# Who loads the w_down pieces: one load queue or two in the expert stage of a mixture-of-experts layer

## The chip, the cores and the metric

The kernel runs on one core of a Trainium2 chip. The metric is the device time of one execution in microseconds (us), as the median of several runs.

## What is computed

One decoder layer in f32 for 512 tokens of width 1024: a mixer (matrix-memory heads and a gated MLP that share an input and an output projection), then a mixture of 32 experts, of which every token uses 4, then a final norm. The change lies in the loads of the expert stage alone:

```
xb  = x[toks]                          # the tokens of one block of one expert
hb  = xb @ w_up[e] + b_up[e]           # 1024 -> 2048
act = min(glu,7) * sigmoid(1.702*glu) * (clip(lin,-7,7) + 1)
yb  = (act @ w_down[e] + b_down[e]) * gate      # 1024 -> 1024
y[toks] += yb
```

Each expert has 12.58 MB of weights (w_up 8.39 MB, w_down 4.19 MB), all of which are read from HBM once: 403 MB in total.

## The kernel before

The mixer and the router take the first 310 us or so. Then the tokens are cut into blocks of 32 rows by expert; an expert that has n tokens takes ceil(n/32) blocks, and at least one. For the inputs of this case there are 78 blocks.

**The order of experts.** Two weight buffers W0 and W1 in SBUF take turns; the text calls the turn of an expert its *position*, 0 to 31, and its buffer is the position's parity `par`. Experts 0 and 1 stand at positions 0 and 1 (their weights are loaded before the router is done). The others are sorted by load on VectorE, and light and heavy ones alternate, the most uneven pairs first. A table `order_tab` holds the expert of each position, `base_tab` the number of blocks before it. In blocks the positions hold 3, 2, 1, 5, 1, 4, 1, 4, 1, 4, 2, 3, then 2 and 3 in turn up to position 27, and 2, 2, 2, 1 at the end (counted in the trace: one L1047 per block, one L1089 per position).

**Pieces.** A weight buffer is cut into six pieces of 2 MB (128 partitions of 16 KB): pieces 0 to 3 are w_up, here called u0 to u3, pieces 4 and 5 are w_down, here d4 and d5. `load_piece` (L299 to L307) issues one; it lands on its own semaphore `s_w[par][n]`. `load_bias_up` (L309) and `load_bias_dn` (L314) load 8 KB and 4 KB of bias.

**TensorE (L1366 to L1414).** `block_up` does 64 matmuls (L1376) that need u0 to u3 in turn, and tells with `m_u[0..3]` when each piece has been read. `block_down` does 64 matmuls (L1391) for the block before it; after the first half it counts `m_yh` (d4 has been read), after the second `m_y` (d5 has been read). The order on TensorE is up(g), down(g-1), up(g+1), down(g), also across experts: the last block of one expert does its down part behind the first up part of the next.

**VectorE (L1041 to L1100).** Per block it adds the bias (L1047, counts `m_z`), clips, multiplies, transposes; L1064 adds the down bias out of PSUM, L1066 multiplies by the gate and counts `m_ys`. L1078 transposes the next block's tokens. **ScalarE (L670 to L672)** does one sigmoid a block: it waits for `m_gl` from L1049. **GpSimd (L499 to L539)** gathers the tokens of a coming block (L506) and scatters the result of the last (L515), both as indirect DMAs of 128 KB.

**SyncE issues every weight load, in one order (L384 to L402).** For each position from 2 on it goes through the pieces 0 to 5. Before each it waits until the former user of the buffer has read that piece (`m_u`, `m_yh`, `m_y`), before the biases also for `m_z` and `m_ys`, and from the third piece on for the landing of the piece two before it (`AHEAD = 2`):

```
for n in range(6):
    sp.wait_ge((*m_u, m_yh, m_y)[n], done)
    ...
    if n >= AHEAD:
        sp.wait_ge(s_w[par][n - AHEAD], 16 * i + 16)
    load_piece(sp, par, n, e)
```

At the end SyncE loads the residual rows (L411), waits for the last scatter, loads all results (L415), and the four tiles of 128 tokens are summed, normed and stored.

Of the kernel before, what the change touches and what calls it, by code (L numbers as in the profile page):

```python
# [30 lines left out]
ALU = mybir.AluOpType  # L31
ACT = mybir.ActivationFunctionType
# [10 lines left out]
NE = 32  # L43
TOPK = 4
BT = 32
NBMAX = T * TOPK // BT + NE
# [4 lines left out]
ALPHA = 1.702  # L51
# [4 lines left out]
def hybrid_layer(nc, x, norm1_gain, w_in, conv_qk, b_igate, b_fgate, mlstm_norm_gain, gmlp_ln_gain,  # L56
# [3 lines left out]
    with ctx:  # L60
# [31 lines left out]
        order_tab = sb("order_tab", [P, NE], i32)  # L92
        base_tab = sb("base_tab", [P, NE + 3], i32)
# [12 lines left out]
        z = m(512)  # L106
        sg, aT = m(256), m(256)
# [205 lines left out]
        def load_bias_dn(eng, par, e):  # L313

            src = b_down[0, e].rearrange("e (j c) -> (e j) c", j=H)
            eng.dma_start(bias_dn[par][0:P:BT, :], src).then_inc(s_bd[par], 16)
# [4 lines left out]
        @block.sync  # L321
        def _(sp):
            def load_x(c):
                sp.dma_start(xin[:, c, :], x[0, P * c:P * (c + 1), :]).then_inc(s_tile[c], 16)

            def load_group(slot, c0):
                sp.dma_start(grp[slot], wcols(c0)).then_inc(s_grp[slot], 16)

            load_x(0)
            load_x(1)  # L330
            load_group(VG, 1024)
            load_x(2)
            load_x(3)
            load_group(QG, 0)
            sp.wait_ge(s_const, 5)
            sp.dma_start(wg[:, :, 0:8], w_in[0, :, 2048:2056].rearrange("(k p) n -> p k n", p=P)).then_inc(s_wg, 16)
            for slot, c0 in ((KG, 512), (OG, 1536), (VGG, 2568), (UG, 2056)):
                load_group(slot, c0)
            sp.wait_ge(s_proj, 12)
            sp.dma_start(wo, w_out[0].rearrange("(k p) n -> p k n", p=P)).then_inc(s_wo, 16)  # L340
            sp.wait_ge(s_wt, NT)
            sp.dma_start(n2row, norm2_gain.broadcast_to([P, D])).then_inc(s_n2row, 16)
            sp.wait_ge(s_proj, 24)
            for c in range(NT):
                sp.dma_start(xres[:, c, :], x[0, P * c:P * (c + 1), :]).then_inc(s_xres, 16)

            def first(par, n):
                load_piece(sp, par, n, slice(par, par + 1))

            first(0, 0)  # L350
            first(0, 1)
            sp.wait_ge(s_p, NT * H)
            sp.wait_ge(s_hm, NT)
            sp.wait_ge(s_hg, NT)
            first(1, 1)
            for c in range(NT):
                if c == NT - 2:
                    sp.wait_ge(s_hTe, 2 * NT)
                    first(0, 5)
                if c == NT - 1:  # L360
                    sp.wait_ge(s_out, 2 * NT)
                    first(0, 2)
                    sp.wait_ge(s_bz, 1)
                    for par in range(2):
                        load_bias_up(sp, par, slice(par, par + 1))
                        load_bias_dn(sp, par, slice(par, par + 1))
                sp.wait_ge(s_hs, c + 1)
                rows = slice(P * H * c, P * H * (c + 1))
                sp.dma_start(hres[rows, :].rearrange("(p j) n -> p (j n)", j=H), xres[:, c, :]).then_inc(s_rowst[c], 16)
                sp.dma_start(hsrow[rows, :].rearrange("(p j) n -> p (j n)", j=H), HS[:, c % 2, :])\  # L370
                    .then_inc(s_rowst[c], 16)
            first(0, 3)
            sp.wait_ge(s_lge, NT)
            first(1, 5)
            for c in range(NT):
                sp.wait_ge(s_rowst[c], 32)
            first(0, 4)
            first(1, 0)
            first(1, 4)
            sp.wait_ge(s_gtab, 1)  # L380
            sp.wait_ge(s_trash, 32)
            first(1, 2)
            first(1, 3)
            with sp.Fori(1, NE // 2) as i:  # L384
                for par in range(2):
                    e = bass.ts(sp.value_load(order_tab[0:1, bass.ts(2 * i + par, 1)], min_val=0, max_val=NE - 1), 1)  # L386

                    done = sp.value_load(base_tab[0:1, bass.ts(2 * i + (par - 1), 1)], min_val=1, max_val=NBMAX - 1)  # L388
                    for n in range(6):
                        sp.wait_ge((*m_u, m_yh, m_y)[n], done)  # L390
                        sp.nop(nofuse=True)
                        if n == 1:
                            sp.wait_ge(m_z, done)
                            sp.nop(nofuse=True)
                            load_bias_up(sp, par, e)
                        if n == 4:
                            sp.wait_ge(m_ys, done)
                            sp.nop(nofuse=True)
                            load_bias_dn(sp, par, e)
                        if n >= AHEAD:  # L400
                            sp.wait_ge(s_w[par][n - AHEAD], 16 * i + 16)
                        load_piece(sp, par, n, e)  # L402

            done = sp.value_load(base_tab[0:1, NE - 1:NE], min_val=1, max_val=NBMAX - 1)
            sp.wait_ge(m_y, done)
            sp.nop(nofuse=True)
            sp.dma_start(grow, final_gain.rearrange("(a n) -> a n", a=1).broadcast_to([P, D]))\
                .then_inc(s_late, 16)
            for c in range(NT):
                rows = slice(P * H * c, P * H * (c + 1))  # L410
                sp.dma_start(hfin[:, c, :], hres[rows, :].rearrange("(p j) n -> p (j n)", j=H)).then_inc(s_tile[c], 16)  # L411
            sp.wait_ge(f_ready, 1)
            for c in range(NT):
                rows = slice(P * H * TOPK * c, P * H * TOPK * (c + 1))
                sp.dma_start(yfin[:, c, :], yrow[rows, :].rearrange("(p r) n -> p (r n)", r=H * TOPK))\  # L415
                    .then_inc(s_tile[c], 16)
            for c in range(NT):
                sp.wait_ge(f_y, c + 1)
                sp.dma_start(out[0, P * c:P * (c + 1), :], hfin[:, c, :]).then_inc(f_out, 16)
            sp.wait_ge(f_out, 16 * NT)  # L420
# [129 lines left out]
        def _(act):  # L550
# [116 lines left out]

            act.wait_ge(s_tab, 1)
            total = act.value_load(base_tab[0:1, NE:NE + 1], min_val=NE, max_val=NBMAX - 1)
            with act.Fori(0, total) as g:  # L670
                act.wait_ge(m_gl, g + 1)
                act.activation(sg, z[:, 0:256], ACT.Sigmoid, scale=ALPHA).then_inc(m_sg, 1)  # L672

            for c in range(NT):
                act.wait_ge(f_sum, c + 1)
# [6 lines left out]
        def _(dve):  # L682
# [251 lines left out]
            for c in range(NT):  # L934
                residual(c, 0)
                if c + 1 < NT:
                    cat_evac(c + 1)
                if c >= 1:
                    norm_evac(c - 1)
                    top_experts(c - 1)  # L940
                residual(c, 1)
                if c == NT - 1:
                    norm_evac(c)
                second_norm(c)
                if c == 0:
                    dve.wait_ge(s_rc, 8)
                    V.tensor_copy(iota_f, iota_i)
                    V.tensor_copy(iota16, iota_i)
                    V.tensor_copy(tokm, tokm_i)
                    V.tensor_copy(spread16, ident[0:BT, 0:BT].unsqueeze(1).broadcast_to([BT, H, BT]))  # L950
                    V.tensor_copy(spread, ident[0:BT, 0:BT].unsqueeze(1).broadcast_to([BT, H, BT]))
                    V.tensor_scalar(part_i[:, 1:2], part_i[:, 0:1], 5, None, ALU.logical_shift_right)
                    link(V.tensor_scalar(part_i[:, 2:3], part_i[:, 0:1], 31, None, ALU.bitwise_and))
                    link(V.tensor_copy(partf[:, 1:3], part_i[:, 1:3]))
                    link(V.tensor_scalar(partf[:, 3:4], partf[:, 1:2], float(T * TOPK * H), None, ALU.add))
                    V.tensor_scalar(partf[:, 2:3], partf[:, 2:3], float(H), None, ALU.mult)
                    link(V.tensor_copy(partf[:, 0:1], part_i[:, 0:1]))
                    link(V.tensor_scalar(late[:, 1:2], partf[:, 0:1], 1.5, 4096.0, ALU.is_lt, ALU.mult))
                    V.tensor_tensor(late[:, 1:2], late[:, 1:2], partf[:, 0:1], ALU.subtract)
                    link(V.tensor_scalar(expb, ones, partf[:, 0:1], None, ALU.mult))  # L960
            top_experts(NT - 1)

# [145 lines left out]
            def base(e):  # L1108

                return dve.value_load(base_tab[0:1, bass.ts(e, 1)], min_val=1, max_val=NBMAX - 1)  # L1110
# [335 lines left out]
```

## Time and profile before

| | us |
|---|---|
| median of 3 runs | 1337.59 (1337.36 to 1339.75) |
| the profiled execution | 1336.38 |
| its span in the profile | 1334.5 |
| TensorE matmul busy | 1140.2 (85%) |
| VectorE busy | 489.4 (37%) |
| ScalarE busy | 200.0 (15%) |
| GpSimd busy | 225.2 (17%) |
| moved by DMA | 463.78 MB |

Times within the trace are us from the start of the span. A line as L306 is a line of the kernel before. "SPq" rows are DMA issues on SyncE's queue; the time beside such a row with "x2" or "x3" runs from the first issue of the group to the end of the last, waits between them included. "GB/s" is what all 16 DMA engines moved, and the DMA share is the mean busy share of these engines. Of all DMA queues the one of SyncE is q1 and GpSimd's is q0; ScalarE's is q10.

### The profile page before, as it was taken

Reading aid. Unit: us, or ns where it says so; the run is one execution under the profiler, and the core shown is the slowest. Engines: PE = TensorE matmul, PEld = TensorE weight load, DVE = VectorE, ACT = ScalarE, POOL = GpSimd, SP = SyncE. Lnnn points to the kernel's source line nnn. Section 1 sums busy time; section 2 is a strip of 40 time slices with the busy share of each in tenths; the row PEclk is TensorE's granted clock in tenths of the full one; section 3 lists DMA queues with packets and bytes.
Section 4 is the critical chain, followed back from the end, with each engine's and each line's share of the span. In section 5 each row is a group of like instructions: output and inputs, shape, how many; then the busy total and the mean of one; then the engine's idle time right before and its main releaser. Section 6 shows DMA issues by size and latency. Waiting matters only on the chain.

```text
span 1334.5 us, 28532 instructions
## 1 busy us (share of the span) xinstructions
PE 1140.2 (85%) x10978; PEld 526.0 (39%) x10979; DVE 489.4 (37%) x1224; ACT 200.0 (15%) x297; POOL 225.2 (17%) x392
## 2 busy tenths in 40 slices
PE   7999999976979997979998979879798989798740
PEld 3445554543434442433443424333333434343220
DVE  2283462443323332433433323333332333233217
ACT  2114321011111111111111111111111111111101
POOL 2000022001112221212221212121221212121113
PEclk9999999986989998999999999998998999998885
DMA  9303005349699999999999999999999999999987
GB/s 346 117 1 126 16 1 225 153 174 413 253 414 425 391 425 427 425 427 425 426 425 426 426 427 426 420 424 425 425 426 425 420 428 415 424 426 425 427 352 300
DMA packets 51088, 463.78 MB, mean 348 GB/s; under 512 B 9052, under 2 KB 10264, under 8 KB 25976
## 3 DMA queue, kind: packets, MB, share of 16 engines
q1 hardware_dynamic: 41184, 441.89, 79.4%
q0 software_dynamic: 7632, 20.85, 4.0%
q10 hardware_dynamic: 2248, 0.71, 0.2%
q8 instruction: 16, 0.26, 0.1%
q14 instruction: 8, 0.07, 0.0%
HBM read 446.65 MB, written 16.78 MB: 347 GB/s over the span
## 4 chain that ended last, share of the span: by engine, by line
DMA 56%; PE 29%; SPq 5%; DVE 5%; issue 3%; ACT 0%; POOL 0%; ACTq 0%; POOLq 0%; DVEq 0%
DMA W<-in_w_up_dram 54%; PE B L1151 11%; PE B L1376 8%; PE B L1272 4%; PE B L1391 3%; SPq L306 2%; SPq L311 1%; SPq L386 1%; DMA W<-yrow 1%; SPq L388 1%; DMA yrow<-misc,idx_s 1%; DMA misc<-hsrow,idx_g 1%; DVE W L1123 1%; PE B L1295 0%; PE B L1167 0%
## 5 line engine op out<-in xcount | busy, mean ns | idle before, releaser
L1376 PE MATMUL B<-W,misc 128*32 128x512 f32 x4992 | 590.4, 620 | 117.6 <-DMA W<-in_w_up_dram 82.0
L1376 PEld LDWEIGHTS B<-W,misc 128*32 128x32 f32 x4992 | 184.3, 112 | 473.9 <-issue 464.3
L1391 PE MATMUL B<-W,misc 128*32 128x256 f32 x4992 | 289.7, 383 | 2.5 <-DMA W<-in_w_down_dram 1.6
L1391 PEld LDWEIGHTS B<-W,misc 128*32 128x32 f32 x4992 | 189.6, 112 | 126.9 <-issue 56.0
L1047 DVE TENSOR_TENSOR misc<-B,misc 128x512 f32<-128x512 f32 x78 | 53.9, 691 | 418.5 <-PE B L1376 418.5
L1151 PE MATMUL B<-W 128*128 128x512 f32 x384 | 169.5, 597 | 0.0
L672 ACT ACTIVATE misc<-misc 128x256 f32<-128x256 f32 x78 | 32.5, 416 | 839.8 <-DVE misc L1049 839.8
L503 POOL COPY idx_g<-idx_tab 128x1 uint32 (+1 forms) x79 | 15.0, 190 | 596.5 <-DVE misc L1078 577.7
L1151 PEld LDWEIGHTS B<-W 128*128 128x128 f32 x384 | 72.0, 192 | 84.6 <-issue 84.6
L515 POOL DMA_INDIRECT yrow<-misc,idx_s x78 | 78.4, 1006 | 148.4 <-DVE misc L1066 148.4
L672 ACT ACT_TABLE_LOAD x78 | 100.1, 1283 | 4.8 <-DVE idx_tab L1024 3.5
L506 POOL DMA_INDIRECT misc<-hsrow,idx_g x79 | 77.8, 985 | 62.3 <-POOL idx_g L503 30.1
L1064 DVE TENSOR_TENSOR misc<-B,misc 128x256 f32<-128x256 f32 x78 | 33.0, 423 | 92.9 <-POOL idx_s L511 77.2
L1073 DVE STREAM_TRANSPOSE misc<-misc 128x256 f32<-128x256 f32 x78 | 34.6, 444 | 69.9 <-PE B L1391 69.9
L1272 PE MATMUL B<-W 128*128 128x512 f32 x128 | 57.8, 609 | 0.1
L1055 DVE TENSOR_TENSOR misc<-misc 128x256 f32<-128x256 f32 x78 | 48.5, 622 | 2.7
L1272 PEld LDWEIGHTS B<-W 128*128 128x128 f32 x128 | 24.5, 195 | 29.6 <-issue 29.6
L443 POOL TENSOR_SCALAR misc<-misc 128x1 f32<-128x1 f32 (+1 forms) x20 | 5.3, 264 | 173.7 <-ACT W L639 80.4
L1078 DVE STREAM_TRANSPOSE misc<-misc 128x256 f32<-128x256 f32 x79 | 33.5, 423 | 2.0 <-DMA misc<-hsrow,idx_g 2.0
L1052 DVE SCALAR_TENSOR_TENSOR misc<-misc 128x256 f32<-128x256 f32 x78 | 33.2, 425 | 2.7
L1066 DVE TENSOR_SCALAR misc<-misc,gate_tab 128x256 f32<-128x256 f32 x78 | 27.6, 353 | 11.0
L1049 DVE TENSOR_SCALAR misc<-misc 128x256 f32<-128x256 f32 x78 | 22.9, 294 | 2.7
(267 smaller groups left out, 487.0 us busy)
## 6 DMA issues: line engine op xcount, KB each, us to landing
W<-in_w_up_dram SPq DMA_DIRECT2D x128, 2048.0 KB, 11.6
W<-in_w_down_dram SPq DMA_DIRECT2D x64, 2048.0 KB, 9.8
W<-in_w_in_dram SPq DMA_DIRECT2D x6, 2048.0 KB, 18.9
W<-yrow SPq DMA_DIRECT2D x4, 2048.0 KB, 14.7
W<-in_x_dram SPq DMA_DIRECT2D x8, 512.0 KB, 5.0
W<-in_w_out_dram SPq DMA_DIRECT2D x1, 4096.0 KB, 12.8
hres<-W SPq DMA_DIRECT2D x4, 512.0 KB, 3.1
hsrow<-W SPq DMA_DIRECT2D x4, 512.0 KB, 4.0
```

Source lines behind the costliest of these rows:

```text
L506: pool.indirect_dma_start(out=xg, out_offset=None, in_=hsrow, in_offset=bass.IndirectOffsetOnAxis(ap=idx_g[:, 0:1], axis=0))\
L515: pool.indirect_dma_start(out=yrow, out_offset=bass.IndirectOffsetOnAxis(ap=idx_s[:, 0:1], axis=0), in_=ysb, in_offset=None).then_inc(m_sc ...
L672: act.activation(sg, z[:, 0:256], ACT.Sigmoid, scale=ALPHA).then_inc(m_sg, 1)
L1047: V.tensor_tensor(z, B[0][:], bias_up[par], ALU.add).then_inc(m_z, 1)
L1052: V.scalar_tensor_tensor(lin, lin, 1.0, glu, ALU.add, ALU.mult).then_inc(m_t, 1)
L1055: V.tensor_tensor(glu.rearrange("p (m r i) -> p m i r", m=2, r=4), lin.rearrange("p (m i r) -> p m i r", m=2, r=4), sg.rearrange("p (m i r ...
L1073: V.transpose(aT, z[:, 0:256]).then_inc(m_aT, 1)
L1078: V.transpose(xT, xg).then_inc(m_xT, 1)
L1151: ins = mm(B[n % 2][:], lhs(k), rhs(k), start=(k == 0), stop=(k == NK - 1))
L1272: ins = mm(B[n][:], HT[:, c % 2, k, :], wo[:, k, 512 * n:512 * (n + 1)], start=(k == 0), stop=(k == NK - 1))
L1376: ins = mm(B[0][BT * j:BT * (j + 1), :].rearrange("p (g h c) -> p g h c", g=2, h=2), xT[:, BT * k:BT * (k + 1)], up(par)[:, k, :, :, P * j ...
L1391: ins = mm(B[5][BT * j:BT * (j + 1), 0:QC], aT[:, BT * q:BT * (q + 1)], down(par)[:, q, QC * j:QC * (j + 1)], start=(q == 0), stop=(q == N ...
```

## The change

SyncE keeps pieces 0 to 3 and the up bias. ScalarE issues pieces 4 and 5 and the down bias on its own queue, between its sigmoids, without the wait for an earlier piece's landing. For this its one loop over all blocks is cut into one loop per position. The rule that sorts the experts on VectorE gets two other operations in place of two, which also order experts 0 and 1 among themselves; for these inputs it gives the same order.

```diff
-                    for n in range(6):
-                        sp.wait_ge((*m_u, m_yh, m_y)[n], done)
+                    for n in range(4):
+                        sp.wait_ge(m_u[n], done)
                         sp.nop(nofuse=True)
                         if n == 1:
                             sp.wait_ge(m_z, done)
                             sp.nop(nofuse=True)
                             load_bias_up(sp, par, e)
-                        if n == 4:
-                            sp.wait_ge(m_ys, done)
-                            sp.nop(nofuse=True)
-                            load_bias_dn(sp, par, e)
                         if n >= AHEAD:
                             sp.wait_ge(s_w[par][n - AHEAD], 16 * i + 16)
                         load_piece(sp, par, n, e)
...
-            with act.Fori(0, total) as g:
-                act.wait_ge(m_gl, g + 1)
-                act.activation(sg, z[:, 0:256], ACT.Sigmoid, scale=ALPHA).then_inc(m_sg, 1)
+            def base(e):
+                return act.value_load(base_tab[0:1, bass.ts(e, 1)], min_val=1, max_val=NBMAX - 1)
+            def sigmoids(first, last):
+                with act.Fori(first, last) as g:
+                    act.wait_ge(m_gl, g + 1)
+                    act.activation(sg, z[:, 0:256], ACT.Sigmoid, scale=ALPHA).then_inc(m_sg, 1)
+            sigmoids(0, base(1) + 1)
+            with act.Fori(1, NE // 2) as i:
+                for par in range(2):
+                    e = bass.ts(act.value_load(order_tab[0:1, bass.ts(2 * i + par, 1)], min_val=0, max_val=NE - 1), 1)
+                    done = base(2 * i + (par - 1))
+                    act.wait_ge(m_yh, done)
+                    act.nop(nofuse=True)
+                    load_piece(act, par, 4, e)
+                    act.wait_ge(m_y, done)
+                    act.nop(nofuse=True)
+                    load_piece(act, par, 5, e)
+                    act.wait_ge(m_ys, done)
+                    act.nop(nofuse=True)
+                    load_bias_dn(act, par, e)
+                    sigmoids(done + 1, base(2 * i + par) + 1)
...
-                    link(V.tensor_scalar(late[:, 1:2], partf[:, 0:1], 1.5, 4096.0, ALU.is_lt, ALU.mult))
-                    V.tensor_tensor(late[:, 1:2], late[:, 1:2], partf[:, 0:1], ALU.subtract)
+                    link(V.tensor_scalar(late[:, 1:2], partf[:, 0:1], -2.0, 0.0, ALU.add, ALU.min))
+                    V.scalar_tensor_tensor(late[:, 1:2], late[:, 1:2], -4096.0, partf[:, 0:1], ALU.mult, ALU.subtract)
```

On SyncE's queue, one even position (buffer W0) before; s_w0_0 to s_w0_3 are the landings of u0 to u3 of this position:

```order
L306 ISA [waits m_u0]
L306 DMA W0<-in_w_up_dram 128x4096
L311 ISA [waits m_u1,m_z]
L311 DMA misc<-in_b_up_dram 4x4x128
L306 ISA
L306 DMA W0<-in_w_up_dram 128x4096
L401 ISA [waits m_u2]
L306 ISA [waits s_w0_0]
L306 DMA W0<-in_w_up_dram 128x4096
L306 ISA [waits m_u3,s_w0_1]
L306 DMA W0<-in_w_up_dram 128x4096
L316 ISA [waits m_yh,m_ys]
...
L306 ISA [waits s_w0_2]
L306 DMA W0<-in_w_down_dram 128x4096
L306 ISA [waits m_y,s_w0_3]
L306 DMA W0<-in_w_down_dram 128x4096
```

The up part stays as it is; after its last row SyncE's queue now goes on to the next position's table reads and its wait for m_u0. On ScalarE's queue, the same position in the changed kernel (line numbers of the changed kernel, L675 is the sigmoid):

```order
L306 ISA [waits m_yh]
L306 DMA W0<-in_w_down_dram 128x4096
L306 ISA [waits m_y]
L306 DMA W0<-in_w_down_dram 128x4096
L316 ISA [waits m_ys]
L316 DMA misc<-in_b_down_dram 4x256
...
L669 TENSOR_LOAD base_tab
...
L675 ACTIVATE misc<-misc 128x256 [waits m_gl]
```

The w_down pieces now wait only for the reads of the buffer's former user, and no longer for u2 and u3 of their own position.

## Rows read from the trace of the kernel before

**Rows 1.** Busy time by stretch, all engines.

```profile
core 0: us, PE busy (x) PEld busy (x) DVE busy (x) ACT busy (x) POOL busy (x), PEclk, DMA share, GB/s
351.00:402.00 51.00, 39.75 (x460) 17.22 (x452) 16.02 (x42) 5.95 (x7) 9.48 (x16) 0.93 0.99 404
...
441.00:466.00 25.00, 23.38 (x284) 10.67 (x280) 9.37 (x26) 3.40 (x4) 5.74 (x9) 1.00 0.97 388
...
500.00:1250.00 750.00, 656.72 (x7675) 286.29 (x7668) 250.70 (x638) 101.96 (x120) 142.36 (x240) 0.95 1.01 425
```

**Rows 2.** The DMA queues from 500 to 1250 us.

```profile
q1 hardware_dynamic: 21432, 302.69, 95.3%
q0 software_dynamic: 5813, 15.87, 5.4%
...
W<-in_w_up_dram SPq DMA_DIRECT2D x96, 2048.0 KB, 11.6
W<-in_w_down_dram SPq DMA_DIRECT2D x48, 2048.0 KB, 9.9
```

**Rows 3.** What SyncE's queue waited for: us in total, times, longest.

```profile
SPq L306 <- DMA W<-in_w_up_dram: 695.0, 117, 12.0
...
SPq L398 <- DVE misc L1066: 8.8, 3, 4.2
```

**Rows 4.** ScalarE's wait for its sigmoids, and rows of ScalarE and VectorE, 640 to 650 us.

```profile
ACT misc L672 <- DVE misc L1049: 839.8, 78, 21.4
...
644.39 0.35 DVE L1066 TENSOR_SCALAR misc<-misc,gate_tab 128x256 f32<-128x256 f32 x1
...
650.16 0.42 ACT L672 ACTIVATE misc<-misc 128x256 f32<-128x256 f32 x1 [8.60 <-DVE misc L1049]
```

**Rows 5.** Two table reads on SyncE's queue, their first parts, 371 to 373 us.

```profile
371.76 0.05 SPq L386
...
372.60 0.05 SPq L388
```

**Rows 6.** TensorE at position 3 (five blocks); the last column is idle before, and what ended it.

```profile
402.84 1.92 PE L1376 MATMUL B<-W,misc 128*32 128x512 f32 x16 [2.98 <-DMA W<-in_w_up_dram]
...
408.00 7.08 PE L1376 MATMUL B<-W,misc 128*32 128x512 f32 x64
...
418.32 7.08 PE L1376 MATMUL B<-W,misc 128*32 128x512 f32 x64
...
438.96 7.08 PE L1376 MATMUL B<-W,misc 128*32 128x512 f32 x64
```

**Rows 7.** Issues on SyncE's queue for positions 5 (441.13, 447.01) and 31.

```profile
441.13 0.33 SPq L306 DMA_DIRECT2D W<-in_w_up_dram  x1
447.01 0.64 SPq L311 DMA_DIRECT2D misc<-in_b_up_dram  x1
...
1274.71 5.32 SPq L306 DMA_DIRECT2D W<-in_w_down_dram  x2
```

**Rows 8.** Pieces, all of L306: from issue to landing.

```profile
DMA to landing us min/median/max: 7.9/10.4/26.1
```

**Rows 9.** The chain that ended last, its end: start us, us, what.

```profile
1269.25 10.29 DMA W<-in_w_up_dram
1279.68 1.93 PE B L1376 x16
1281.60 3.49 PE B L1391 x64
1287.15 6.35 DMA yrow<-misc,idx_s
1295.65 2.43 DMA yrow<-misc,idx_s
```

**Rows 10.** The scatters, all of L515: from issue to landing.

```profile
DMA to landing us min/median/max: 2.4/6.9/8.4
```

**Rows 11.** What TensorE waited for, the longest.

```profile
PE B L1376 <- DMA W<-in_w_up_dram: 82.0, 32, 3.8
```

More of the change, by code:

```diff
@@ L669, in _ @@
             total = act.value_load(base_tab[0:1, NE:NE + 1], min_val=NE, max_val=NBMAX - 1)
-            with act.Fori(0, total) as g:
-                act.wait_ge(m_gl, g + 1)
-                act.activation(sg, z[:, 0:256], ACT.Sigmoid, scale=ALPHA).then_inc(m_sg, 1)
+            def base(e):
[19 more added lines that the diff above has]
+                    sigmoids(done + 1, base(2 * i + par) + 1)
+            behind_last = base(NE - 1)
+            with act.If_lt(act.to_reg(behind_last + 1), act.to_reg(total)):
+                sigmoids(behind_last + 1, total)
             for c in range(NT):
```

## The prediction

> **What bounds the kernel now.** I read the busy time by stretch first, then the DMA queues, then the waits, then the chain. From 500 to 1250 us the 16 DMA engines are busy for the whole time at 425 GB/s, while TensorE has 657 of 750 us [rows 1]. In that stretch SyncE issues 96 pieces of w_up and 48 of w_down [rows 2]: 750/144 = 5.21 us a piece, 31.3 us a position, whatever TensorE does. TensorE waits for pieces of w_up, 32 times and 82.0 us in all [rows 11]. So the reader should see a stream of 180 pieces (positions 2 to 31) that is the clock of the stage, and compute that hangs on it. SyncE itself is no bound: 695.0 us of its queue's time are waits for a landing [rows 3].
>
> Two places matter more than that average. The first is **the end**. The chain runs through u3 of position 31, which lands at 1279.54 (1269.25 + 10.29), then the last quarter of the up part (1279.68), a down part (1281.60), and two scatters (1287.15 and 1295.65) [rows 9]. d5 of position 31 is issued only at about 1279.7, behind the landing of u3 (the second of the pair that starts at 1274.71) [rows 7], and lands while the chain goes through TensorE and the first scatter. So the last two pieces of the stream are not on the path; the last u3 is. The second is **position 3**, the expert with five blocks. Its u3 lets TensorE go on at 402.84; four more blocks follow, the last up part from 438.96, one block each 10.32 us (418.32 - 408.00) [rows 6]. Only when that last up part has read u0 can SyncE issue u0 of position 5, at 441.13 [rows 7].
>
> **The change, part by part.**
>
> *SyncE loses two pieces, a bias and their waits.* Its waits for m_ys were 8.8 us in three cases [rows 3]. All of that stands beside a DMA stream that is full; worth 0. If the cover went, the most it could give back is what the stream lacks where it is not full: 51 us at 404 instead of 425 GB/s and 25 us at 388 [rows 1], that is 51 x 0.05 = 2.5 and 25 x 0.09 = 2.2, together 4.7 us.
>
> *ScalarE gets 30 times two pieces, a bias and three table reads.* An issue takes 0.33 us on SyncE's queue and a bias 0.64 [rows 7]; a read of a table takes 0.84 us (372.60 - 371.76 [rows 5]). The bias goes behind m_ys, counted by L1066 (644.39 + 0.35); with 0.64 and one read ScalarE is free at 646.2, and its next sigmoid starts at 650.16 after 8.60 us of idle [rows 4]. The rest is done earlier. ScalarE's idle before its sigmoids is 839.8 us for 78 [rows 4], 10.8 us each. Cost 0, with 4 us of cover at each position. The table load of 1.28 us behind each sigmoid goes from the loops; it stood in the same idle time, so 0. VectorE's two exchanged operations on one column each, once: 0.
>
> *The order of the stream changes.* This is the main term. Before, d4 waits for the landing of u2 and d5 for that of u3, so the stream is u0 u1 u2 u3 d4 d5 in each position. After, ScalarE issues d4 of position p+2 when TensorE has done half a down part behind position p+1's first up part. That is 1.9 + 1.7 us after u3 of p+1 has landed (the last quarter of the up part and half of a down part's 3.49 [rows 9]), and d5 1.7 us later. At that time SyncE can have at most u0 and u1 of p+2 on its queue; u2 must wait until u0 has landed, a piece time later. So both d pieces are with the engines before u2 and u3 are. The scatters show how the engines treat two queues: a scatter of 128 KB lands after 2.4 us when nothing else runs, and mostly after 6.9 us beside the weights [rows 10], although whole pieces need 7.9 us at the least [rows 8] and several are queued. It isn't put behind them all; the queues take turns. With turns, both d pieces need at most 4 x 5.21 = 20.8 us from their issue and are in before u3. **u3 becomes the last piece of its position**, 2 x 5.21 = 10.4 us later for the same bytes moved. The Trainium skill ("DMA: Bandwidth & Descriptors", section "Queues, rings and completion order") says that each DMA engine goes round-robin between the queues that have work, packet by packet; the scatters' landing agrees.
>
> At the end this is paid in full: the chain hangs on the last u3, so **+10.4 us**. The bounds are 0 (d pieces still behind u3) and 10.4.
>
> *Position 3 runs the stream dry.* From the landing of u3 (402.84) to the issue of u0 of position 5 (441.13) are 38.3 us, set by TensorE. Before, eight pieces stand between the two (d4 d5 of position 3, six of position 4): 8 x 5.21 = 41.7 us. A piece alone takes 7.9 us from issue to landing [rows 8], 7.9 - 4.9 = 3.0 more than its 2.1 MB at 425 GB/s. 38.3 + 3.0 = 41.3 is just under 41.7: the stream holds, nearly, which is what the 0.97 share there shows [rows 1]. After, d4 and d5 of position 3 are already in, and six pieces remain: 31.3 us. The engines idle for 41.3 - 31.3 = **+10.0 us**. The positions with four blocks (5, 7, 9) free the buffer 10.3 us earlier: 41.3 - 10.3 = 31.0 against 31.3, no dry time, but no margin either. Those with three or fewer have 10 us to spare. Bounds: 0 (order as before) and 10.0 + 3 x 2 = 16, if each four-block position misses by 2 us (its u1 still waits for m_z behind u0: 447.01 against 441.13 is 5.9 us, more than a piece [rows 7]).
>
> *The tail gets lighter.* In the changed kernel nothing of the weights is behind the last u3. The first scatter of the tail took 6.35 us beside d5, the last 2.43 [rows 9], so up to 3.9 us may come back; but the loads of the residual rows, which stood behind d5, now run beside it. I take half: **-2**, bounds -3.9 and 0.
>
> *Gathers and scatters share with a third queue.* One scatter to the next is its landing plus 2.15 us (1295.65 - 1287.15 - 6.35 [rows 9]); with the usual 6.9 [rows 10] that is 9.05 against a block of 10.32 [rows 6], a margin of 1.27 us. One busy weight queue adds 4.5 us (6.9 - 2.4) to a landing. The trace has no stretch with two; the nearest row bounds what the second adds by 0 and 4.5. Where TensorE waits for weights anyway it costs nothing; only the blocks behind the first ones of the heavy positions feel it. I take **+1**, close to the lower end, since most of the stage has slack on TensorE.
>
> **Sum.** 10.4 + 10.0 - 2 + 1 = 19.4 us, made against the profiled execution's 1336.38; the median is 1.2 us above that: 1337.6 + 19.4 = **1357**. The case's own range is 1351 to 1368: below, the third term at -3.9, the fourth at 0, and 3 us off because the d pieces only partly get ahead; above, the second at 16, the third at 0, the fourth at 4.5 (1337.6 + 10.4 + 16 + 4.5).
>
> **Rivals.**
>
> *Faster.* The engines serve SyncE's queue so that the w_up pieces aren't held up by ScalarE's, and ScalarE's pieces fill the holes of the stream, at 351 to 402 and 441 to 466 us: 4.7 us as worked out, 1333. It decides if u3 of a position keeps landing before its d5. For it: the stream has those holes, and SyncE stands at waits in one fixed order. Against it: d4 and d5 are issued before u2 is, and the total is 425 GB/s with or without a second queue beside it (q1 and q0 give 95.3% and 5.4% [rows 2]), so more queues bring no more rate.
>
> *No change.* The stream is full, nothing else changes, and the last d pieces stay off the path: 1337.6, within the 0.2% (2.7 us) that a measurement of this kernel can tell. The Trainium skill, same page, section "Issuing engines are not separate DMA queues", says that starting DMAs from several engines saves only the sequencer's time to initiate them; by that rule alone this rival would be the forecast. What speaks against it is that the order changes, which that rule says nothing of.
>
> *Only the end.* The stream doesn't run dry at position 3, because SyncE issued something I don't see or the d pieces of positions 3 and 4 come late: 1337.6 + 10.4 - 2 = 1346.
>
> *The indirect transfers become the bound.* If the second queue adds the full 4.5 us, a block takes 6.9 + 4.5 + 2.15 = 13.55 us wherever ScalarE's queue is busy, 3.2 more than now. Over the 17 blocks of positions 3, 5, 7 and 9 that is up to 55 us, over the four later blocks of position 3 alone 13; between these I take 25: 1382. It decides above 1.27 us of extra landing time. For it: the margin is that thin. Against it: TensorE has slack behind position 10.
>
> **Chances.** Forecast 0.64, only the end 0.11, indirect transfers 0.12, faster 0.08, no change 0.05. The range takes in forecast and "only the end", and the half of the indirect case that costs less: 1344 to 1376, with 0.08 + 0.05 + 0.07 left out. Faster by over 0.2%: 0.08; within: 0.05; slower: 0.87.
>
> **What would show it.** Right: DMA issues on ScalarE's queue, each d pair issued before its u2; the wait of TensorE for w_up grown; a stretch of about 10 us between 430 and 460 us in which the DMA share falls to near 0; then 425 GB/s again; the last u3 landing at about 1300, with no weight landing after it, and 53 us from there to the end. Wrong: the DMA share at position 3 unbroken (second term), d5 landing behind the last u3 (first term), or the scatters' median landing above 8.2 us with blocks apart by more than 10.3 us (fourth term). A rate other than 425 GB/s in the middle would upset the whole sum: each per cent is 9 us.

## The result, and the profile after

| | before | changed |
|---|---|---|
| median of 4 runs, us | 1337.47 (1336.98 to 1339.75) | 1357.21 (1356.79 to 1357.39) |
| ratio, 95% interval | | 1.0145 (1.0129 to 1.0162) |
| span of the profiled execution | 1334.5 | 1355.6 |

The changed kernel is slower by 19.7 us, where 19.4 were forecast. First its busy time by stretch (columns as in rows 1: us, PE, PEld, DVE, ACT, POOL, TensorE's clock, DMA share, GB/s):

```profile
351.00:402.00 51.00, 38.13 (x440) 16.44 (x432) 16.11 (x42) 1.83 (x4) 9.45 (x16) 0.93 1.00 410
402.00:441.00 39.00, 32.34 (x364) 12.82 (x368) 11.07 (x27) 1.25 (x3) 5.42 (x10) 0.87 1.00 420
441.00:466.00 25.00, 23.84 (x288) 9.70 (x284) 8.96 (x22) 0.83 (x2) 6.41 (x11) 1.00 0.55 201
...
500.00:1250.00 750.00, 658.61 (x7744) 285.14 (x7739) 252.18 (x639) 24.99 (x60) 143.47 (x243) 0.94 1.01 425
```

From 500 to 1250 us the rate has not changed: 425 GB/s as in [rows 1], with the weights on two queues now instead of one. Between 441 and 466 us the DMA share fell from 0.97 to 0.55, 201 GB/s instead of 388: (0.97 - 0.55) x 25 = 10.5 us of the stream lost. Nearly all of it lies between 440 and 452 us, where the share is 0.14:

```profile
440.00:452.00 12.00, 12.00 (x148) 4.86 (x144) 4.22 (x11) 0.42 (x1) 3.54 (x6) 1.00 0.14 53
```

The page's DMA queues show how the weights are divided, and its DMA issues how long a piece now takes from issue to landing (median, last column):

```profile
q1 hardware_dynamic: 32304, 315.94, 56.3%
q10 hardware_dynamic: 11128, 126.66, 22.1%
...
W<-in_w_up_dram SPq DMA_DIRECT2D x128, 2048.0 KB, 18.7
W<-in_w_down_dram ACTq DMA_DIRECT2D x60, 2048.0 KB, 23.2
```

In [rows 2] these medians are 11.6 and 9.9 us, from 500 to 1250 us; in the same stretch of the changed kernel they are 19.4 and 20.5 us. The two queues share the engines, and each piece takes about twice as long. The end of the chain that ended last (start us, us, what):

```profile
1253.15 25.17 DMA W<-in_w_up_dram
1278.47 20.80 DMA W<-in_w_up_dram
...
1299.40 3.64 PE B L1398 x16
1303.05 3.62 PE B L1413 x64
...
1308.73 5.97 DMA yrow<-misc,idx_s
...
1316.85 2.44 DMA yrow<-misc,idx_s
```

The last u3 lands at 1299.27 (1278.47 + 20.80), against 1279.54 in [rows 9]: 19.7 us later. The spans of the two profiled executions differ by 21.1 us (1355.6 - 1334.5); the 1.4 us left over lie behind that landing. (The profiled execution before was 1.1 us shorter than its median, the changed one 0.2 us longer, so the medians differ by 19.7.) No weights move any more from 1299 us on, as the busy time of the next 5 us shows (DMA share 0.00, the column before the last):

```profile
1299.00:1304.00 5.00, 4.60 (x36) 1.69 (x40) 0.86 (x2) 0.00 (x0) 0.18 (x1) 0.58 0.00 0
```

TensorE at position 3, to be read against [rows 6] (L1398 is the up part, L1413 the down part; in brackets the idle time before, and what ended it):

```profile
405.23 3.64 PE L1398 MATMUL B<-W,misc 128*32 128x512 f32 x16 [7.96 <-DMA W<-in_w_up_dram]
412.30 3.59 PE L1398 MATMUL B<-W,misc 128*32 128x512 f32 x16 [3.42 <-DMA W<-in_w_up_dram]
415.69 3.66 PE L1413 MATMUL B<-W,misc 128*32 128x256 f32 x64
419.16 7.05 PE L1398 MATMUL B<-W,misc 128*32 128x512 f32 x64
...
429.48 7.05 PE L1398 MATMUL B<-W,misc 128*32 128x512 f32 x64
...
450.12 7.05 PE L1398 MATMUL B<-W,misc 128*32 128x512 f32 x64
```

u3 of position 3 lets TensorE go on at 412.30 instead of 402.84, 9.5 us later. The last of the five up parts starts 37.8 us after that (450.12 - 412.30; before 438.96 - 402.84 = 36.1). The difference of 1.7 us is the last quarter of the first up part, 3.59 us here and 1.92 before. Only then can u0 of position 5 be issued:

```profile
452.27 0.34 SPq L306 DMA_DIRECT2D W<-in_w_up_dram  x1
```

That is 40.0 us after 412.30, and in this time the stream has six pieces to carry instead of eight.

### The profile page after: what moved, and what is told of

The parts are those of the page before. It is cut to its first block, busy times and chain, and to the rows that moved or that the text cites. A ratio compares the mean times of both kernels' runs of the same rounds, so it can differ in the third digit from the quotient of the medians.

```text
span 1355.6 us, 28875 instructions
## 1 busy us (share of the span) xinstructions
PE 1138.5 (84%) x10978; PEld 519.0 (38%) x10979; DVE 491.2 (36%) x1224; ACT 105.1 (8%) x224; POOL 224.5 (17%) x392
## 4 chain that ended last, share of the span: by engine, by line
PE 53%; DMA 38%; DVE 5%; issue 1%; SPq 1%; ACT 0%; POOL 0%; ACTq 0%; POOLq 0%; DVEq 0%
DMA W<-in_w_up_dram 34%; PE B L1398 24%; PE B L1173 11%; PE B L1413 11%; PE B L1294 4%; DMA W<-in_w_down_dram 2%; DMA W<-yrow 1%; DVE misc L1069 1%; SPq L311 1%; DMA yrow<-misc,idx_s 1%; DMA misc<-hsrow,idx_g 1%; DVE W L1145 0%; DMA W<-in_b_spatial_dram 0%; PE B L1317 0%; PE B L1189 0%
## 5 line engine op out<-in xcount | busy, mean ns | idle before, releaser
L1398 PE MATMUL B<-W,misc 128*32 128x512 f32 x4992 | 585.4, 619 | 134.7 <-DMA W<-in_w_up_dram 98.3
L1398 PEld LDWEIGHTS B<-W,misc 128*32 128x32 f32 x4992 | 182.2, 113 | 485.8 <-issue 475.6
L1413 PE MATMUL B<-W,misc 128*32 128x256 f32 x4992 | 293.0, 386 | 5.1 <-DMA W<-in_w_down_dram 4.2
L1413 PEld LDWEIGHTS B<-W,misc 128*32 128x32 f32 x4992 | 184.9, 113 | 140.3 <-issue 65.2
L675 ACT ACTIVATE misc<-misc 128x256 f32<-128x256 f32 x78 | 32.5, 417 | 955.6 <-DVE misc L1071 955.6
L507 POOL COPY idx_s<-misc 128x1 uint32 (+1 forms) x78 | 14.8, 189 | 60.3 <-DMA yrow<-misc,idx_s 60.0
## 6 DMA issues: line engine op xcount, KB each, us to landing
W<-yrow SPq DMA_DIRECT2D x4, 2048.0 KB, 14.6
```

Source lines behind the costliest of these rows:

```text
L1398: ins = mm(B[0][BT * j:BT * (j + 1), :].rearrange("p (g h c) -> p g h c", g=2, h=2), xT[:, BT * k:BT * (k + 1)], up(par)[:, k, :, :, P * j ...
L1413: ins = mm(B[5][BT * j:BT * (j + 1), 0:QC], aT[:, BT * q:BT * (q + 1)], down(par)[:, q, QC * j:QC * (j + 1)], start=(q == 0), stop=(q == N ...
```

## The experiments

Times below are medians; each ratio is to the kernel before on the same chip, with its 95% interval. A difference of two ratios is turned into us with 1338. A single ratio is good to between 1.4 and 3.6 us by its interval, so the differences to the changed kernel under the next two headings are each good to about 4 us. The runs have names (e1 to e10); the "first" and the "sixth experiment" of an expectation are e1 and e6.

### e2: position 31 alone goes back to SyncE

In this and the next two kernels the body of each loop over positions is a function, and the first and the last pair of positions are written out, so that one position can differ; the rest is the changed kernel.

```diff
+        SYNC_DOWN = (31,)
...
+                for n in range(pieces):
+                    sp.wait_ge((*m_u, m_yh, m_y)[n], done)
...
-                    for n in range(4):
-                        sp.wait_ge(m_u[n], done)
...
+            load_position(NE // 2 - 1, 0, 4)
+            load_position(NE // 2 - 1, 1, 6 if 31 in SYNC_DOWN else 4)
...
+            position(NE // 2 - 1, 0, True)
+            position(NE // 2 - 1, 1, 31 not in SYNC_DOWN)
```

The third argument is the number of pieces that SyncE loads, and on ScalarE whether it loads w_down.

> The changed kernel, but at position 31 alone SyncE issues d4 and d5 behind u2 and u3, as before. Theory (the last u3 is the end of the path): 10.4 us less than the changed kernel, 1346 to 1348, the last u3 landing at about 1289, the dry stretch at position 3 unchanged. Rival (only the total of the stream counts, the order at the end is hidden): 1357, no change.

Measured: 1349.14 us, ratio 1.0074 (1.0048 to 1.0101). Against the 1.0145 of the changed kernel that is 0.0071 x 1338 = 9.5 us less, a little short of the 10.4 that was expected. The dry stretch is as it was (0.55). The chain of this kernel:

```profile
1248.13 20.84 DMA W<-in_w_up_dram
1269.11 3.64 PE B L1419 x16
1272.75 4.18 PE B L1434 x64
1276.93 6.87 PE B L1419 x64
1283.80 3.45 PE B L1434 x64
...
1287.77 7.07 PE B L1419 x64
1294.84 3.49 PE B L1434 x64
```

The chain no longer ends in the u3 of position 31, but in that of position 30 (1248.13 + 20.84 = 1268.97), from where TensorE works with hardly a break (0.5 us): u0 to u3 of position 31 are in before it comes to them. So the order at the end does cost time, and what is next behind the last u3 is the u3 of position 30, late for the same reason. That the 10.4 us show as 9.5 fits this, but the difference is less than these times can tell.

### e3: position 3 alone goes back to SyncE

```diff
+        SYNC_DOWN = (3,)
...
+            load_position(1, 1, 6 if 3 in SYNC_DOWN else 4)
...
+            position(1, 1, 3 not in SYNC_DOWN)
```

> The changed kernel, but at position 3 alone (five blocks) SyncE issues d4 and d5 behind u2 and u3. Theory: the stream no longer runs dry at position 3, the DMA share from 441 to 466 us goes from 0.55 back to 0.95 or more, and 10 us go: 1346 to 1349. Rival (the dry stretch only moves to another heavy position, or was hidden in TensorE's slack): 1354 to 1357.

Measured: 1347.91 us, ratio 1.0068 (1.0043 to 1.0092), 0.0077 x 1338 = 10.3 us less than the changed kernel. Its busy time by stretch:

```profile
402.00:441.00 39.00, 38.04 (x464) 15.56 (x468) 14.40 (x35) 1.67 (x4) 7.25 (x13) 0.96 1.01 424
441.00:466.00 25.00, 23.27 (x286) 9.80 (x280) 9.63 (x25) 0.83 (x2) 5.91 (x10) 1.00 0.93 371
```

TensorE is busy for 38.0 of 39 us again (32.3 in the changed kernel), and the DMA share is back at 0.93, a little under the 0.95 that was expected. The rival fell. No run has the first and last pairs written out with nothing moved back; that this alone changes nothing is argued from the traces (e2 keeps the dry stretch, e3 the late last u3) and from the next run.

### e4: both go back to SyncE

```diff
+        SYNC_DOWN = (3, 31)
```

> The changed kernel with d4 and d5 of positions 3 and 31 on SyncE, behind u2 and u3; the other 28 positions stay on ScalarE. Theory: both terms go and they add: 1336 to 1340, the time of the kernel before. Rival (the second queue costs something of its own all along, through slower scatters and gathers): 1341 to 1347 remain.

Measured: 1338.40 us, ratio 0.9998 (0.9988 to 1.0009). Two of 30 positions moved back, and the whole loss is gone: 9.5 + 10.3 = 19.8 against 19.7. The other 28 positions keep the second queue, with all that it does to gathers and scatters, and cost nothing that can be measured (the interval reaches 1.6 us below the kernel before and 1.2 us above it). Their stretch still reads 425 GB/s:

```profile
500.00:1250.00 750.00, 656.37 (x7744) 287.40 (x7740) 253.93 (x641) 25.06 (x60) 143.62 (x243) 0.95 1.01 425
```

### e5: turns or age

```diff
-        AHEAD = 2
+        AHEAD = 4
```

> The changed kernel with AHEAD = 4: SyncE issues u0 to u3 as soon as the buffer's former user has read them, with no wait for an earlier landing. In light positions all four are then issued before ScalarE's d4 and d5. If the engines take turns between the two queues: the d pieces still get half the rate and are in before u3, so 1355 to 1358, as the changed kernel. If they serve by age of issue: u3 lands ahead of d4 and d5 in the light positions, the last u3 about 10 us earlier, 1344 to 1350.

Measured: 1358.65 us, ratio 1.0149 (1.0128 to 1.0171): as the changed kernel. The issues for position 31, SyncE's and then ScalarE's (the third of the three up pieces ends at 1255.38):

```profile
1253.91 1.47 SPq L306 DMA_DIRECT2D W<-in_w_up_dram  x3
```

```profile
1275.60 1.78 ACTq L306 DMA_DIRECT2D W<-in_w_down_dram  x2
```

and the chain:

```profile
1255.05 45.10 DMA W<-in_w_up_dram
1300.28 3.64 PE B L1398 x16
```

u3 was issued 20 us ahead of d4 and landed 45 us after its issue, at 1300.15, at the end of the stream. Had the engines served by age, it would have been in before both d pieces. Service by age is ruled out: the two queues take turns. But d5 isn't in before u3 either, as the expectation had it: it was issued at 1277.03 and landed 23.3 us later, at 1300.3. Both queues run out together. The Trainium skill ("DMA: Bandwidth & Descriptors", section "Queues, rings and completion order") says that an engine goes round between the queues that have work; by it the time stays, and the run agrees.

### e1 and e7: one queue in the new order

```diff
-                    for n in range(6):
+                    turn = (0, 1, 4, 5, 2, 3)
+                    for k, n in enumerate(turn):
...
-                        if n >= AHEAD:
-                            sp.wait_ge(s_w[par][n - AHEAD], 16 * i + 16)
+                        if k >= AHEAD:
+                            sp.wait_ge(s_w[par][turn[k - AHEAD]], 16 * i + 16)
```

> The kernel before, with SyncE alone issuing everything, but in the order u0 u1 d4 d5 u2 u3 in each position; ScalarE issues nothing. Theory (the order of the stream is the cause): u3 is again the last piece of its position, so about 10 us at the end and about 10 us dry time at position 3 come as in the changed kernel: 1354 to 1359, the DMA share between 441 and 466 us near 0.55, the last u3 landing at about 1299. Rival (the second queue is the cause: turns between queues, ScalarE's issues, slower gathers and scatters): 1337 to 1340.

Measured: 1456.33 us, ratio 1.0886 (1.0859 to 1.0912). Neither theory gave this number. What SyncE's queue waited for (us in total, times, longest; L1392 is the down part, L1067 counts m_ys):

```profile
SPq L392 <- PE B L1392: 308.9, 30, 11.6
...
SPq L399 <- DVE misc L1067: 128.3, 30, 7.0
```

SyncE now stands at m_yh and m_ys in each of the 30 positions with only u0 and u1 queued, 10.4 us of work, for (308.9 + 128.3) / 30 = 14.6 us on average, and the stream runs dry: from 500 to 1250 us its DMA share is 0.94 and it moves 387 GB/s. The next run, e7, took the wait for m_ys away from there, by putting the down bias behind u3.

```diff
-                        if n == 4:
-                            sp.wait_ge(m_ys, done)
-                            sp.nop(nofuse=True)
-                            load_bias_dn(sp, par, e)
...
                         load_piece(sp, par, n, e)
+                    sp.wait_ge(m_ys, done)
+                    sp.nop(nofuse=True)
+                    load_bias_dn(sp, par, e)
```

> As the first experiment (SyncE alone, order u0 u1 d4 d5 u2 u3), but the down bias with its wait for m_ys goes behind u3 instead of ahead of d4. If that run's extra 100 us came from SyncE standing at m_ys with only two pieces queued behind it, the wait gone leaves the order alone: the DMA share from 500 to 1250 us is back at 1.0, and the time is 1354 to 1362. If waiting for m_yh and m_y alone is enough to drain two pieces: 1380 to 1450.

Measured: 1399.16 us, ratio 1.0440 (1.0413 to 1.0467), 405 GB/s in that stretch. So the wait for m_ys was about half of it (118 us lost with it, 59 without), and the waits for m_yh and m_y drain the queue by themselves:

```profile
SPq L392 <- PE B L1391: 343.7, 55, 12.0
```

These two don't separate order from queue, since a second mechanism came in: on one queue a late wait holds back every piece behind it. So no run shows the new order without the second queue; what speaks against the second queue as the cause is e4, in which 28 positions keep it at no cost. What e1 and e7 do show is what ScalarE's own queue is good for: with w_down issued between u1 and u2 one queue costs 59 us, while the two queues cost 20.

### e8, e6, e9 and e10: SyncE's waits, and the tail

```diff
-        AHEAD = 2
+        AHEAD = 4
```

> The kernel before with AHEAD = 4 instead of 2. If SyncE's landing waits leave holes in the stream (it is idle for 3.2 us between 356 and 1280 us in the kernel before), 1335 to 1337; if the stream is full whatever SyncE does, 1337 to 1339; if a deeper queue slows gathers and scatters, above 1339.

Measured: 1338.32 us, ratio 0.9997 (0.9983 to 1.0011). The stream is full with SyncE's landing waits or without most of them.

The other edit to the kernel before moves the residual rows behind the last scatter:

```diff
-            for c in range(NT):
-                rows = slice(P * H * c, P * H * (c + 1))
-                sp.dma_start(hfin[:, c, :], hres[rows, :].rearrange("(p j) n -> p (j n)", j=H)).then_inc(s_tile[c], 16)
             sp.wait_ge(f_ready, 1)
             for c in range(NT):
...
                     .then_inc(s_tile[c], 16)
+                rows = slice(P * H * c, P * H * (c + 1))
+                sp.dma_start(hfin[:, c, :], hres[rows, :].rearrange("(p j) n -> p (j n)", j=H)).then_inc(s_tile[c], 16)
```

> The kernel before, with the four loads of the residual rows issued behind the last scatter, each behind the result rows of its tile, instead of ahead of it. If these loads hold up the two scatters of the tail: the first of them lands after 2.4 to 4 us instead of 6.35, the end comes 1 to 3 us earlier, 1334.5 to 1337. If d5 alone holds it up: the scatter stays at 6 us and the result rows come up to 1.2 us later for it, 1338 to 1340.

Measured: 1337.86 us, ratio 1.0003 (0.9989 to 1.0017), no gain. Its profile is read from e9, the same kernel once more.

> The kernel of the sixth experiment once more, for its profile. If the residual rows hold up the first scatter of the tail, it lands after 2.4 to 4 us; if d5 does, after 6 us or more. The time as there, 1335 to 1339.

Measured once: 1338.79 us. The first scatter of the tail (L514) and what follows it on GpSimd:

```profile
1289.99 0.99 POOL L514 DMA_INDIRECT yrow<-misc,idx_s  x1 [11.70 <-DVE misc L1065]
1292.72 0.18 POOL L510 COPY idx_s<-misc 128x1 uint32 x1 [1.73 <-DMA yrow<-misc,idx_s]
```

It landed within 2.7 us of its issue, against 6.35 in [rows 9]: in the kernel before, too, it was mainly the residual rows that held it up. (d5 was still in flight for about 1 us of it here and 2.4 us there.) The chain now goes through d5, which has come onto the path:

```profile
1281.26 9.70 DMA W<-in_w_down_dram
...
1291.10 1.97 PE B L1390 x32
...
1294.77 2.44 DMA yrow<-misc,idx_s
```

The same edit to the changed kernel:

> The changed kernel with the same edit: the residual rows behind the last scatter. No weight is behind the last u3 here, so the first scatter of the tail has the engines for itself: it lands after 2.4 to 3 us instead of 5.97, the end comes 2 to 3 us earlier than the changed kernel, 1354 to 1355.5. If the scatter stays at 6 us something else than the loads holds it up, and the time is 1357 to 1359.

Measured: 1359.01 us, ratio 1.0159 (1.0143 to 1.0176), not faster than the changed kernel; the 2 to 3 us that were expected to go did not. The chain:

```profile
1310.28 2.45 DMA yrow<-misc,idx_s
...
1314.88 2.43 DMA yrow<-misc,idx_s
...
1321.12 24.93 DMA W<-hres
1346.08 2.30 DVE W L1144
```

The scatter does land in 2.45 instead of 5.97 us: the residual rows were what it shared with. But these 3.5 us are given back: the residual rows are now loaded together with the result rows, and the last of them lands at 1346.05, where the last result rows of the changed kernel land at 1342.25. No version tried here beats the kernel before.

## Why the prediction was right, point by point

**What bounds the kernel: right.** 425 GB/s before and after, and 426 with a deeper queue (e8). The Trainium skill ("DMA: Bandwidth & Descriptors", section "Issuing engines are not separate DMA queues") says that the issuing engines share the same 16 DMA engines, and the rate agrees; its conclusion, that only issue time is saved, would have given no change. The order that pieces land in is what it leaves out.

**u3 becomes the last piece: right in what it costs at the end, wrong in its picture.** The step had both d pieces "with the engines before u2 and u3", and in before u3, after 20.8 us at most. Position 31 of the changed kernel: u2, then d4 and d5, then d5 alone with its time from issue to landing:

```profile
1273.48 0.33 SPq L306 DMA_DIRECT2D W<-in_w_up_dram  x1
```

```profile
1274.88 1.57 ACTq L306 DMA_DIRECT2D W<-in_w_down_dram  x2
```

```profile
1276.11 0.34 ACTq L306 DMA_DIRECT2D W<-in_w_down_dram  x1
```

```profile
DMA to landing us min/median/max: 23.3/23.3/23.3
```

d4 was issued 1.4 us behind u2 and 3.6 us ahead of u3 (1278.47), and d5 landed at 1299.4, 0.2 us behind u3 (1299.27). So two signs came out against the prediction: "each d pair issued before its u2", and "d5 landing behind the last u3", which it had named as a sign that the term is wrong. Nor was position 31 an exception: of the 30 positions, d4 was issued ahead of u2 in 7, and d5 landed behind u3 in 20. d4 came later than the step had it, 6.4 us instead of 3.6 us after the landing of the u3 before (1268.48 in this trace). 1.7 us of that are the quarter in between, which took 3.64 us behind a wait of 7.33 (see the last section); what makes up the rest stays open.

What holds is less than the step said, and enough: from 1275 us on u2 and u3 share the engines with d4 and d5, so the last u3 is not in before the whole stream is. Before, it was in two pieces, 10.4 us, ahead of the end of the stream. 10.4 is thus the most that the term can be, and both queues ran out together, so that it was reached. The prediction took this bound for a reason that the trace doesn't bear out; in so far its size is luck. Undone alone (e2) the term measured 9.5 us.

**Position 3 runs dry: right.** 10.0 us forecast. Lost in that stretch: 10.5 us by the DMA share; undone alone (e3): 10.3. Of the 19.7 us by which the last u3 lands later, 19.7 - 10.4 = 9.3 are left for it. Here d4 and d5 are in before u3 (409.7 and 412.2 us), as the first step had it. It left out that TensorE needs 40.0 instead of 38.3 us from there to the release of u0, 1.7 us more, the slower quarter behind the wait; by its own sum that makes 40.0 + 3.0 - 31.3 = 11.7. That 41.3 against 41.7 us is only just enough before, and 31.0 against 31.3 for four blocks after, held too: the DMA share is 1.01 from 500 to 1250 us, where the buffers of positions 5, 7 and 9 come free.

**The tail gets lighter: wrong.** -2 us was forecast. From the landing of the last u3 to the end of the span are 1355.6 - 1299.27 = 56.33 us, against 1334.5 - 1279.54 = 54.96: +1.4. The first scatter takes 5.97 instead of 6.35 us, because it shares with the residual rows (e10, and e9 for the kernel before), hardly with d5; and the last quarter of the up part takes 3.64 instead of 1.93 us (see the last section), which the prediction did not have. The step "up to 3.9 us may come back" took d5 for what the scatter shares with.

**Gathers and scatters: +1 us was forecast, and nothing of it can be seen.** All scatters of the changed kernel, from issue to landing:

```profile
DMA to landing us min/median/max: 2.4/8.7/11.4
```

The median is 1.8 us above [rows 10], over the 8.2 that was named as a warning and beyond the margin of 1.27. Yet 28 positions with the second queue cost nothing in e4. The other half of that warning did not come: the blocks behind the first of position 3 are 10.32 us apart (429.48 - 419.16), as before, although d4 and d5 of position 4 were issued on ScalarE's queue at 419.08 and landed at 434.6 and 443.0. The longest scatter of all, 11.4 us, lies in this stretch. So the prediction's rule, that a landing plus 2.15 us must fit into one block, does not hold for a single scatter. How many late ones in a row it would take, no run shows.

**The other costs at 0: right.** ScalarE's busy time fell from 200.0 to 105.1 us, because the table load behind each sigmoid went, and this moved nothing; its waits before the sigmoids are 955.6 us now.

**The sum.** Forecast 10.4 + 10.0 - 2 + 1 = 19.4, measured 19.7. The two main terms carry it: 9.5 + 10.3 by the experiments (each good to about 4 us), 0.0147 x 1338 = 19.7 for both together (e4, good to about 3). That the sum is right to 0.3 us is luck. Between the two profiles the last u3 moved by 19.7 us where 20.4 were forecast and the tail by +1.4 where it was -2, a miss of 3.4; the +1 us for gathers and scatters did not show; and of the 21.1 us that this makes, the medians show 19.7, since the profiled execution before was a short one.

## What to carry to other kernels

When one stream of loads is the clock of a stage, count what each consumer needs last. Moving a part of the loads to another queue added no rate here (425 GB/s either way); the queues take turns, and the pieces that were last and off the path now share the engines with those that are on it, which land later for it. Before such a move, look at the two places where the stream has a boundary: its end (what lands last, and does the chain wait for it?), and the longest stretch in which no buffer comes free (how many pieces are queued for it, against how long it lasts).

A single queue with mixed conditions is no free answer either: pieces whose release comes late must stand behind enough others. Two pieces of 5.2 us were too few here for waits of 14.6 us on average (e1, m_yh and m_ys together).

## What the runs showed of the hardware that was not expected

**TensorE's clock after a wait.** Before, TensorE waited 3.8 us at most for a piece [rows 11]; after, less often and up to 8.0:

```profile
PE B L1398 <- DMA W<-in_w_up_dram: 98.3, 20, 8.0
```

The last quarter of the last up part, 16 matmuls, took 1.93 us before and 3.64 after. Before, the granted clock was 1.00 there:

```profile
1279.00:1284.00 5.00, 4.32 (x65) 2.56 (x69) 2.24 (x6) 0.42 (x1) 0.00 (x0) 1.00 1.01 433
```

After, it is 0.58 from 1299 to 1304 us, so that the engine ran in part at 1.2 instead of 2.4 GHz. Ahead of it the engine had stood still for 7.34 us:

```profile
1299.40 3.64 PE L1398 MATMUL B<-W,misc 128*32 128x512 f32 x16 [7.34 <-DMA W<-in_w_up_dram]
```

At position 3 the two waits of 7.96 and 3.42 us had the same behind them, 3.64 and 3.59 us; before, 1.92 us followed a wait of 2.98 [rows 6]. Where the stream is the clock of the stage this costs nothing. Where TensorE is, it does: 1.7 us at the end, and 1.7 us at position 3, where it decides when u0 is released.

**A second busy queue and small transfers.** A scatter of 128 KB took 2.4 us alone (the last of the tail), 6.9 (median) beside one busy weight queue and 8.7 beside two at least part of the time. The second queue adds 1.8 us where the first adds 4.5, so the cost isn't one fixed amount for each queue.
